# Local attention's probabilities transposed by VectorE's 32x32 blocks and moved within SBUF instead of by TensorE

## The reference

```python
def hybrid_layer(x, g, w_in, rpb, w_dw, b_dw, ln_g, ln_b, w_pw, b_pw, w_out, pos):
    h = rms_norm(x, g)
    z = h @ w_in
    aq, ak, av, ag, bq, bk, bv, bg, ca, cb, cg = jnp.split(z, splits, axis=-1)
    ya = neighbourhood_attention(aq, ak, av, rpb) * silu(ag)          # 4 heads of 64, window 8 rows x 16 columns
    yb = dilated_attention(rotary(bq), rotary(bk), bv) * silu(bg)     # 6 heads of 64
    yc = conformer_conv(ca, cb, w_dw, b_dw, ln_g, ln_b, w_pw, b_pw) * silu(cg)
    return x + concatenate([ya, yb, yc], axis=-1) @ w_out
```

## Time and profile before

| | |
|---|---|
| median of 3 runs | 534.11 us (533.26 to 535.69) |
| profiled execution, its own time | 536.4 us |
| its span (first to last instruction) | 534.4 us |
| mean granted TensorE clock | 0.994 |
| busy: TensorE, VectorE, ScalarE, GpSimd | 98%, 69%, 52%, 25% |
| DMA traffic | 94.41 MB, 38917 packets |

### The profile page before, as it was taken

How to read it: one execution, slowest core, us unless ns; L and a number is a source line. 1 busy time by engine, 2 the same in 40 slices (tenths; PEclk the granted TensorE clock), 3 DMA queues, 4 the chain that set the end, 5 groups by cost and what they waited for, 6 DMA issues and landing times.

```text
span 534.4 us, 7774 instructions
## 1 busy us (share of the span) xinstructions
PE 521.7 (98%) x2846; PEld 407.1 (76%) x2846; DVE 370.1 (69%) x721; ACT 279.5 (52%) x535; POOL 136.2 (25%) x168
## 2 busy tenths in 40 slices
PE   8999999999999999999999999999999999999985
PEld 6888777586786878888888877767768687878764
DVE  6989797989984544612639969989999447553044
ACT  6713375565765575634423317665766566663123
POOL 0104332122142312335211323132213242223101
PEclk9999999999999999999999999999999999999988
DMA  8625787867675984899303569967676679699953
GB/s 286 264 79 147 164 197 182 169 162 169 139 199 131 237 172 103 201 282 262 127 0 109 129 144 223 229 148 175 144 178 149 181 186 216 178 232 261 254 98 157
DMA packets 38917, 94.41 MB, mean 177 GB/s; under 512 B 5088, under 2 KB 16608, under 8 KB 38624
## 3 DMA queue, kind: packets, MB, share of 16 engines
q0 software_dynamic: 17856, 61.09, 51.2%
q1 hardware_dynamic: 20736, 32.64, 19.4%
q10 hardware_dynamic: 288, 0.19, 0.1%
HBM read 83.94 MB, written 6.82 MB: 170 GB/s over the span
## 4 chain that ended last, share of the span: by engine, by line
PE 71%; DVE 11%; DMA 10%; issue 3%; ACT 1%; SPq 1%; POOL 1%; POOLq 0%; DVEq 0%; ACTq 0%
PE acc L562 16%; PE acc L564 16%; PE acc L563 16%; PE tp L686 5%; DMA w_hi<-w_out 4%; DMA sq<-sq 4%; PE sc L672 3%; PE misc L705 3%; DVE ub L1208 2%; DVE y L1208 2%; DMA w_lo<-w_out 2%; SPq L465 1%; DVE prob L1228 1%; PE sc L562 1%; PE sc L564 1%
## 5 line engine op out<-in xcount | busy, mean ns | idle before, releaser
L562 PE MATMUL acc<-act_hi,w_hi 128*128 128x512 f32 x480 | 195.3, 407 | 0.0
L564 PE MATMUL acc<-act_lo,w_hi 128*128 128x512 f32 x480 | 187.7, 391 | 0.0
L563 PE MATMUL acc<-act_hi,w_lo 128*128 128x512 f32 x480 | 187.4, 390 | 0.0
L564 PEld LDWEIGHTS acc<-act_lo,w_hi 128*128 128x128 f32 x480 | 90.1, 188 | 20.0
L562 PEld LDWEIGHTS acc<-act_hi,w_hi 128*128 128x128 f32 x480 | 90.3, 188 | 17.8 <-issue 1.4
L563 PEld LDWEIGHTS acc<-act_hi,w_lo 128*128 128x128 f32 x480 | 90.4, 188 | 16.9 <-issue 0.5
L785 ACT ACTIVATE w_lo<-w_hi 128x1024 fp32r<-128x1024 f32 (+1 forms) x62 | 62.0, 1000 | 50.9 <-DMA w_hi<-w_out 46.3
L848 ACT ACTIVATE prob<-prob,nmx 128x512 f32<-128x512 f32 (+1 forms) x80 | 50.4, 630 | 38.3 <-DVE nmx L1228 38.3
L1208 DVE SCALAR_TENSOR_TENSOR y<-ub,par,y 128x512 f32<-128x512 f32 x90 | 67.7, 752 | 0.0
L1208 DVE SCALAR_TENSOR_TENSOR ub<-ub,par 128x512 f32<-128x512 f32 x84 | 65.8, 783 | 0.0
L873 ACT ACTIVATE pT<-tp 128x512 f32<-128x512 f32 (+1 forms) x80 | 40.1, 502 | 45.3 <-PE tp L686 45.3
(11 more groups left out here) (143 smaller groups left out, 719.6 us busy)
## 6 DMA issues: line engine op xcount, KB each, us to landing
w_hi<-w_in POOLq DMA_DIRECT2D x40, 512.0 KB, 5.4
w_lo<-w_in POOLq DMA_DIRECT2D x40, 512.0 KB, 6.0
w_hi<-w_out POOLq DMA_DIRECT2D x16, 512.0 KB, 7.5
w_lo<-w_out POOLq DMA_DIRECT2D x16, 512.0 KB, 7.0
pT<-w_in SPq DMA_DIRECT2D x15, 512.0 KB, 5.2
bias<-nabias SPq DMA_DIRECT2D x32, 128.0 KB, 3.2
sq<-sq SPq DMA_DIRECT2D x48, 64.0 KB, 3.1
v_way<-vB SPq DMA_DIRECT2D x8, 256.0 KB, 2.5
```

Of the source, the lines that this page charges most:

```text
L562: nc.tensor.matmul(to[:, :], w_hi[:, slot, k, :], a_hi[:, k, :], start=i == 0, stop=False)
L563: nc.tensor.matmul(to[:, :], w_lo[:, slot, k, :], a_hi[:, k, :], start=False, stop=False)
L564: last = nc.tensor.matmul(to[:, :], w_hi[:, slot, k, :], a_lo[:, k, :], start=False, stop=i == K - 1)
```

## The change

1. The probabilities of the local units are no longer transposed by TensorE. They stand in four places of 256 columns in the first half of `prob` (`p_of`). VectorE transposes their 32x32 blocks (`turn_p`, unit n in slot n + 2) into a buffer for a **batch** of four units: the second half of `prob` for batches 0 and 2, `sq` for 1 and 3 (`p_turned`). SyncE then issues 16 DMAs for each batch, of 32 partitions x 256 elements (32 KB), straight to their place in pT (`move_p`, `P_MOVES`). `turn_p` of batches 2 and 3 first waits until batch 0 or 1 has landed, since it uses the same buffer.
2. `values` of pair 3 goes from slot 34 to the end of slot 39 and waits for the moves of batches 0 and 1. `values` of pair 4 waits for batches 2 and 3. In layer 0 it stands behind the first 21 matmuls of the first w_out tile; the last three matmuls of the first two tiles are done after those of both (`K_ORDER` ends in 7, 1). In layer 1 it stands before the fourth row part.
3. x's blocks are moved within SBUF too, 16 DMAs of 64 KB for each half (`move_x`) in place of a store and four loads: the first half turned in slot 26 and issued in slots 27 to 30, the second half issued when the products of the first half are done.

```diff
-K_ORDER = [2, 3, 4, 0, 5, 6, 1, 7]
+K_ORDER = [2, 3, 4, 0, 5, 6, 7, 1]
+        P_MOVES = {30: [(0, 0)], 31: [(0, 1)], 32: [(0, 2)], 33: [(0, 3)], 34: [(1, 0)], 35: [(1, 1)],
+                   36: [(1, 2), (1, 3)], 38: [(2, 0), (2, 1)], 39: [(2, 2), (2, 3)]}
+        PV_LOCAL = 39
+        X_BLOCKS = {26: 0}
+        X_MOVES = {27 + i: (0, i) for i in range(QUADS)}
...
+            def move_p(l, q, i):
+                sp.wait_ge(p_blocks, LOCAL * l + BATCH * (q + 1))
+                sp.wait_ge(pv_done, PAIRS * l + DPAIRS)
+                for j in range(QUADS):
+                    sp.dma_start(p_there(q)[BLK * j:BLK * (j + 1), NKEY * i:NKEY * (i + 1)],
+                                 p_turned(q)[BLK * i:BLK * (i + 1), NKEY * j:NKEY * (j + 1)]).then_inc(p_moved[q], 16)
...
+            def move_x(half, i):
+                n = KD // 2 * QT * BLK
                 sp.wait_ge(x_blocks, KD // 2 * (half + 1))
-                sp.dma_start(x_way[half], ub[:, 0:KD // 2 * SEQ]).then_inc(x_stored, 16)
...
+                for i in range(QUADS):
+                    move_p(l, LOCAL // BATCH - 1, i)
                 if l == LAST:
-                    store_x(1)
-                    load_x(1)
+                    sp.wait_ge(tile_done, N_CH * LAST + OUT0 + KD // 2)
+                    for i in range(QUADS):
+                        move_x(1, i)
...
-                pe.wait_ge(pt_ready, UNITS * l + UPP * (g + 1))
+                if g < DPAIRS:
+                    pe.wait_ge(pt_ready, DUNITS * l + UPP * (g + 1))
+                else:
+                    for q in range(UPP // BATCH):
+                        pe.wait_ge(p_moved[UPP // BATCH * (g - DPAIRS) + q], P_MOVED * (l + 1))
...
+                for c in range(N_IN + CT, N_IN + CT + 2):
                     open_tile(l, c)
-                    products(c, act_hi, act_lo, order=K_ORDER, used=act_used if c == N_CH - 1 else None)
+                    products(c, act_hi, act_lo, 0, KD - 1, order=K_ORDER, ready=(ylo_ready, KD * l))
+                    if c == N_IN + CT:
+                        values(l, PAIRS - 1)
+                for c in range(N_IN + CT, N_IN + CT + 2):
+                    products(c, act_hi, act_lo, KD - 1, KD, order=K_ORDER, ready=(ylo_ready, KD * l))
...
+            def turn_p(l, n):
+                dve.wait_ge(p_ready, UNITS * l + n + 1)
+                q, u = divmod(n - DUNITS, BATCH)
+                if n == DUNITS:
+                    dve.wait_ge(t_ready, DUNITS * (l + 1))
+                if u == 0 and q >= 2:
+                    dve.wait_ge(p_moved[q - 2], P_MOVED * (l + 1))
+                to = p_turned(q).rearrange("p (j u h t) -> p u h j t", j=QUADS, u=BATCH, t=BLK)[:, u]
+                nc.vector.transpose(to, p_of(n).rearrange("p (h j t) -> p h j t", j=QUADS, t=BLK)).then_inc(p_blocks, 1)
...
+                    if DUNITS + LAG <= n < UNITS + LAG:
+                        turn_p(l, n - LAG)
```

More of the change, by code:

```diff
@@ L103 @@
 X_GROUPS = [(0, 1), (1, 2), (2, 3), (3, 5), (5, 6), (6, 8)]
-X_ORDER = [list(range(KD))] + [K_ORDER] * (DEPTH - 1)
+X_ORDER = [list(range(KD))] + [[2, 3, 4, 0, 5, 6, 1, 7]] * (DEPTH - 1)
 WARM = 10
@@ L249, in build @@
         p_ready = sem("p_ready")
+        p_blocks = sem("p_blocks")
+        p_moved = [sem(f"p_moved{q}") for q in range(LOCAL // BATCH)]
         t_ready = sem("t_ready")
@@ L531, in _ @@
                         load_v(l, V_LOADS[n])
-                    if l == LAST and n in X_STORES:
-                        store_x(X_STORES[n])
-                    if l == LAST and n in X_LOADS:
-                        load_x(X_LOADS[n])
+                    for q, i in P_MOVES.get(n, ()):
+                        move_p(l, q, i)
+                    if l == LAST and n in X_MOVES:
+                        move_x(*X_MOVES[n])
+                for i in range(QUADS):
+                    move_p(l, LOCAL // BATCH - 1, i)
                 if l == LAST:
-                    store_x(1)
-                    load_x(1)
+                    sp.wait_ge(tile_done, N_CH * LAST + OUT0 + KD // 2)
+                    for i in range(QUADS):
+                        move_x(1, i)
                 if l + 1 < DEPTH:
@@ L680, in turn @@
                 pe.wait_ge(p_ready, UNITS * l + n + 1)
-                if UNITS * l + n:
-                    pe.wait_ge(pt_ready, UNITS * l + n)
-                blocks = QT if g < DPAIRS else NKEY // P
-                for k in range(blocks):
+                if DUNITS * l + n:
+                    pe.wait_ge(pt_ready, DUNITS * l + n)
+                for k in range(QT):
                     last = nc.tensor.transpose(tp[:, k * P:(k + 1) * P],
@@ L708, in values @@
                     for b in range(QT):
+                        there = p_there(UPP // BATCH * (g - DPAIRS) + b // 2).rearrange("p (i u h t) -> p u h i t", i=QUADS,
+                                                                                    u=BATCH, t=BLK)
                         for half in range(2):
@@ L712, in values @@
                                                         v_of(g, i, na_block(b, half)),
-                                                        pT[:, BLK * i // HD, half, b * P:(b + 1) * P],
+                                                        there[:, 2 * (b % 2) + BLK * i // HD, half],
                                                         start=half == 0, stop=half == 1)
@@ L754, in _ @@
                         products(c, s_hi, s_lo)
-                    if n >= UPP + LAG and n % UPP == LAG and n < UNITS + LAG:
+                    if n >= UPP + LAG and n % UPP == LAG and n <= DUNITS + LAG:
                         values(l, n // UPP - 1)
-                    if LAG <= n < UNITS + LAG:
+                    if n == PV_LOCAL:
+                        values(l, DPAIRS)
+                    if LAG <= n < DUNITS + LAG:
                         turn(l, n - LAG)
@@ L764, in _ @@
                         norm_bc(l, MISC_LBC, 2 * l + 2)
-                values(l, PAIRS - 1)
                 if l == LAST:
                     for half, kps in ROW_PARTS:
+                        if (half, kps) == LAST_PAIR:
+                            values(l, PAIRS - 1)
                         row_products(half, kps)
                     break
-                c = N_IN + CT
-                open_tile(l, c)
-                products(c, act_hi, act_lo, order=K_ORDER, ready=(ylo_ready, KD * l))
-                for c in range(N_IN + CT + 1, N_CH):
+                for c in range(N_IN + CT, N_IN + CT + 2):
                     open_tile(l, c)
-                    products(c, act_hi, act_lo, order=K_ORDER, used=act_used if c == N_CH - 1 else None)
+                    products(c, act_hi, act_lo, 0, KD - 1, order=K_ORDER, ready=(ylo_ready, KD * l))
+                    if c == N_IN + CT:
+                        values(l, PAIRS - 1)
+                for c in range(N_IN + CT, N_IN + CT + 2):
+                    products(c, act_hi, act_lo, KD - 1, KD, order=K_ORDER, ready=(ylo_ready, KD * l))
+                for c in range(N_IN + CT + 2, N_CH):
+                    open_tile(l, c)
+                    products(c, act_hi, act_lo, order=X_ORDER[l + 1], used=act_used if c == N_CH - 1 else None)
         @block.scalar
@@ L1361, in _ @@
                         reciprocal(l, n - 1)
-                    if n > UPP + LAG and n % UPP == LAG + 1 and n < SLOTS - 1:
+                    if DUNITS + LAG <= n < UNITS + LAG:
+                        turn_p(l, n - LAG)
+                    if n > UPP + LAG and n % UPP == LAG + 1 and n <= DUNITS + LAG + 1:
                         gated(l, n // UPP - 1)
+                    if n == PV_LOCAL + 1:
+                        gated(l, DPAIRS)
                     j, phase = divmod(n - LN_SILU, 2)
@@ L1422, in row_sum @@
             def row_sum(a, half):
+                if a == 0:
+                    dve.wait_ge(x_moved, X_MOVED * (half + 1))
                 nc.vector.tensor_tensor(by_tile(res[:, 2 * a + half, :]), by_tile(ROW_BANKS[half][a][:, :]),
```

51 lines of the change are left out of this document (26 added, 25 removed).

## The result

The changed kernel took 566.47 us in the median of 6 runs (562.67 to 568.86), the kernel before 534.49 us beside it. The ratio is 1.0574, 95% interval 1.0539 to 1.061: 32 us slower. The forecast was 531.9 and the range ended at 539, so the prediction was wrong, in sign and far outside its range.

The account below looks back on a forecast made before the run. The prediction took TensorE, busy 98% of the span, to bound the kernel. Gains of 7.4, 0.5 and 4.0 us (-11.9) against losses of +9.7 made net -2.2 from 534.11: 531.9 us, range 524 to 539.

Parts of the forecast that it names:

- +9.7: Sum of the forecast's losses: stalls of 0.4 and 1.8 us in slot 34, 5.8 at batch 3, 1.7 of clock.
- The turns' 7.4: TensorE's 32 removed turns of two transposes, 16 a layer, at 0.23 us each: 7.4 us gained.
- the last one's 0.5: The last turn of layer 1 had waited and begun late on TensorE; removing it gains 0.5 us.
- The tail's 4.0: Last projection: TensorE's 2.3 us late start on w_lo and 1.7 us of clock go, 4.0 us gained.
- one loss of clock, 1.7: TensorE's lower clock after a stall costs 1.7 us, charged once, to the 5.8 us stall in layer 0.
- the 12 matmuls behind them cover the gate, y_hi and y_lo: Layer 1, after the last pair's values: 12 matmuls hide the work on their result, so no stall was charged.
- batch 0 in slot 34, +0.4 and +1.8: VectorE waits in slot 34 for batch 0's moves, stalling TensorE 0.4 us in layer 0, 1.8 in layer 1.
- batch 3 in layer 0, +5.8: TensorE waits for batch 3's moves before the last pair's values in layer 0: a 5.8 us stall.
- VectorE stands on batch 0: Rival, chance 0.18: slot 34 in both layers, slow landings; 538.1 us at 4.5 us landing, 544.3 at 6.
- The queue hides: Rival, chance 0.28: cheaper issues or VectorE further ahead leave only 1.3 us at values: 523.5, up to 529 us.
- The weights take the place: Rival, chance 0.10: w_out load late in layer 0, batch 3 fills x's share in layer 1; 536.0 us.
- wrong if: Signs against the forecast: moves issued under 0.5 us, slot 34 holding TensorE over 3 us, w_out's loads late again.

Follow-up runs that it names:

- e4: The kernel before with only x's blocks moved within SBUF, probabilities still turned by TensorE: 531.4 us, ratio 0.9913.
- e8: e4 with the last pair's values among the projection's tiles and ScalarE's order as in the change, no probabilities moved: 545.06 us, ratio 1.0196.
- e11: e8 with one negation (layer 0) or two (layer 1) ahead of ScalarE's last y_hi: 536.33 us, ratio 1.0018.
- e9: The changed kernel with negations ahead of ScalarE's last y_hi and biases in pairs, without moves of probabilities or waits for them: 527.08 us, ratio 0.9833.
- e1: The changed kernel with ScalarE negating two of w_out's tiles before its last y_hi, in both layers: 556.02 us, ratio 1.0369.
- e3: e1 with only one in four of the moves of probabilities, part of the attention left out: 536.44 us, ratio 1.0013.
- e5: The full changed kernel with negations ahead of ScalarE's last y_hi and two units' biases issued together ahead of the moves: 552.39 us, ratio 1.0338.
- e6: e5 with only a quarter of the moves of probabilities, part of the attention left out: 534.6 us, ratio 1.0003.
- e7: e5 with each batch going to DRAM in one store and back in four loads, twice the bytes: 540.71 us, ratio 1.0112.
- e10: e5 with the last pair's v loaded in slot 37 instead of 32: 550.89 us, ratio 1.0271.
- e14: e5 with each four moves of 32 partitions made one of 128, same bytes, output not attention's: 536.69 us, ratio 1.0037.
- e15: e5 with batch 2 turned into zc's space, so that VectorE doesn't wait for batch 0: 550.47 us, ratio 1.0304.

## Why the prediction was wrong

**The sum, remade from the runs,** by the ratios: 534.5; x within SBUF -4.7 (e4); the last pair's values among the projection's tiles +15.1 (e8 less e4), of which 9.5 is ScalarE's order and 5.6 stays without it (e11); the turns -9.9 (e9 less e11; 8.6 in the spans); and what the moves cost, the rest to 566.5, 31.5 (27 where order and biases are mended). The forecast had -4.0, nothing, -7.9 and +9.7. So by size the moves in SyncE's queue failed most, by some 22 us, and the placement by 15.

**Right.** The turns' 7.4 and the last one's 0.5 (7.9, measured 8.6 to 9.9). The tail's 4.0. Transposes hidden on VectorE, strided operand free. The pitch of a move, 0.62: four take 2.42 us with a step of 0.63 (190.87 above). The size of one loss of clock, 1.7 (measured 1.5 to 2.8), though it was charged once and fell five times. The places: slot 34, batch 3 in layer 0, and nothing for batch 3 in layer 1.

**First step that failed: "the 12 matmuls behind them cover the gate, y_hi and y_lo".** It followed the block through VectorE and ScalarE, and not what is queued behind y_hi on ScalarE: the negations of w_out's tiles, the loads that GpSimd issues after them, and TensorE. The 16.8 us that ScalarE stands there could have been worked out before: values moved behind three row parts are 16.3 us later. This is 9.5 to 10.4 us (e8 and e11; e1). The sentence is wrong in itself too. The fourth row part goes from one group of 128 tokens to the next (`row_products`), and each group needs the last pair's block after its first three matmuls. So three matmuls stand ahead of it, not 12, and they don't cover the 2 us of gate, y_hi and y_lo. TensorE's timeline of e1_negate_first, where the weights are there in time:

```profile
517.98 1.95 PE L751 MATMUL misc<-pT,v 128*32 128x128 f32 x64
519.87 0.50 PE L658 MATMUL sc<-w_hi,act_hi 128*128 128x512 f32 x1
520.20 0.40 PE L659 MATMUL sc<-w_lo,act_hi 128*128 128x512 f32 x1
520.44 0.39 PE L660 MATMUL sc<-w_hi,act_lo 128*128 128x512 f32 x1
522.14 0.50 PE L658 MATMUL sc<-w_hi,act_hi 128*128 128x512 f32 x1 [1.31 <-DVE act_lo L1325]
```

The same 1.3 us stand in e3, e5, e6, e7, e9, e10, e11, e14 and e15: a part of what the placement costs with a mended order.

**Second step: batch 0 in slot 34, +0.4 and +1.8.** The forecast let the loads of v follow unit 34's bias at once. They wait for a store that takes 8.37 us to land, 3 us lost in the queue, and batch 0's last move went out at 195.83 rather than 192.5. In layer 1 the sum began x's moves at 429.1; they wait for VectorE's transposes in slot 26 and began at 439.85. Together with issues of up to 2.1 us in a full stretch, batch 0's last move went out at 470.78 where 450.6 was forecast. The wait fell on a bias first, which no step had: every bias of units 32 to 39 stands in the same queue as the moves. TensorE lost 2.18 + 1.44 us in layer 0 and 3.05 + 1.98 + 1.44 in layer 1, and 2.1 and 2.7 us of clock after the two close pairs.

**Third step: batch 3 in layer 0, +5.8.** 4.3 us was measured, but only because everything before it was late as well: the last move was issued at 231.22, not 224.6, and landed 4.8 us later, not 3.0. Where ScalarE's order is mended the wait is 9.6 (e1), and with slot 34's wait gone too it is 9.3 to 10.5 (e15, e10). The term was a wait worked out against an arrival of TensorE that another late step had set; the right quantity was the queue's throughput. In e9_no_moves batch 0 is turned at 175.9 and TensorE begins the last pair's values at 222.0: 46 us. In this time SyncE has 77 issues. By the forecast's own prices (0.62 a move, some 0.4 for the others) they are 45 us, and the last move has yet to land; in e5_order_bias they took 54 us (176.69 to 230.78).

**Of the rivals,** "VectorE stands on batch 0" (0.18) had the mechanism of slot 34, at a fraction of the whole: in the changed kernel VectorE stood on biases there, and on batch 0 once the biases went ahead (e5, e6, e14). "The queue hides" was wrong: a move took 0.62 us to issue. The rule of the Trainium skill that the prediction set beside it (DMA: Bandwidth & Descriptors, Issuing engines are not separate DMA queues) says that the time to initiate a DMA is usually small relative to the DMA. e14_wide_moves speaks against it here: same bytes, a quarter of the issues, 552.4 to 536.7 us. "The weights take the place" was seen as one wait of 2.8 us in layer 0, for a load that took 7.2 us (218.03 in the chain); it was not tried by itself, and the chain leads from its issue back through ScalarE and VectorE to a bias (208.39, 4.20 us to land), so SyncE's queue had a part in it. Of the forecast's "wrong if", two came: slot 34 held TensorE for over 3 us, and w_out's loads were late again, the 8.3 us one by ScalarE's order and not by contention, which nothing in the forecast foresaw.

**What stays open:** what makes up the rest of the 5.6 us that the placement costs with a mended order, beyond the 2.9 us of waits shown, and how much of the moves' 27 us is lost clock rather than waiting, since the clock was counted in the changed kernel alone. Why the medians differ by 6 us more than the two profiled executions was not looked into. A direct test of the queue, a part of the moves issued by another engine, was not made.

## What to carry to other kernels

When a step of one engine is moved later, follow every queue that waits for its result and price what stands behind the waiting instruction there, loads of weights above all; here that was 10 us that no timeline of the moved work shows. When many small DMAs replace a few large ones, sum the issues of the whole stretch, and the landing of the last, against the time that the stretch has, before any single wait is worked out: if the sum is larger, mending one wait only makes the next longer (e5, e10, e15). And price the parts of a change apart: x's moves alone gained 0.9%, with half of the probabilities' moves it was 1.2%, and the whole lost 5.7%.

## What the runs showed of the hardware

A move of 32 partitions within SBUF holds SyncE's queue for 0.63 us when nothing else is in the way, but four took 4.61 us at 180.85 and single issues took up to 2.10 us (450.09, in a window with DMA share 1.05). A full set of DMA engines alone does not explain it: in e5_order_bias eight moves took 4.95 us (0.62 each) from 191.02, with a DMA share of 1.00 from 190 to 200. Landing of the probabilities' moves ran from 1.8 to 6.4 us in the changed kernel, and a 256 KB store to DRAM landed in 2.0 to 8.4 us. A 128x256 block transpose on VectorE takes 0.43 us, more than half of a 128x512 one (0.68). TensorE's granted clock fell to the lower of its two levels in five places, twice behind two waits close together (2.18 and 1.44, 1.98 and 1.44) and three times behind a single one (2.79, 4.31, 8.33), at 1.5 to 2.8 us each, but not after the 3.05 us before 465.24, where the pitch was 0.23 at once.
